# Expert gate and up of a mixture layer: tokens stationary, three passes on halves split on chip, instead of weights stationary in full fp32

## The reference, cut to what matters

```python
def grouped_moe(h, w_router, b_router, w1, w3, w2):      # h: 512 x 1024
    probs = softmax(ht @ w_router)                       # 16 experts
    ...                                                  # two experts and two weights a token
    xs = x_pad[slot_tok].reshape(nblk, MOE_BLOCK, D)     # tokens sorted by expert, padded to blocks
    def expert_block(args):
        xb, e = args
        return (jax.nn.silu(xb @ w1[e]) * (xb @ w3[e])) @ w2[e]
    ys = lax.map(expert_block, (xs, blk_expert)).reshape(P, D) * slot_w[:, None]
    ...                                                  # the two results of a token added
```

## Time and profile before

| | us |
|---|---|
| median of three runs | 3443.12 |
| the profiled execution, its own time | 3443.09 |
| its span from first to last instruction | 3441.1 |
| TensorE busy in the span | 3124.4 (91%) |
| VectorE, ScalarE, GpSimd busy | 1458.3, 1072.6, 1095.8 |
| first product of the expert stage starts, last one ends | 2854.86, 3374.17 |

### The profile page before, as it was taken

How to read it: one execution, slowest core, us unless ns; L and a number is a source line. 1 busy time by engine, 2 the same in 40 slices (tenths; PEclk the granted TensorE clock), 3 DMA queues, 4 the chain that set the end, 5 groups by cost and what they waited for, 6 DMA issues and landing times.

```text
span 3441.1 us, 39144 instructions
## 1 busy us (share of the span) xinstructions
PE 3124.4 (91%) x15510; PEld 2408.1 (70%) x15510; DVE 1458.3 (42%) x2548; ACT 1072.6 (31%) x1673; POOL 1095.8 (32%) x538
## 2 busy tenths in 40 slices
PE   4987999999889789899997999989999968999995
PEld 2664777887666567688775777867777737888883
DVE  6677663212156757332203456647673251000003
ACT  3454324223245432422314442223442230000002
POOL 1331343444323224344443553434543401000001
PEclk8998999999999889999998999999999988999997
DMA  5210553433321036374232226343332308888883
GB/s 210 61 50 25 184 191 104 137 127 94 99 86 51 30 125 206 110 293 135 92 105 79 83 66 243 121 115 110 110 105 86 110 0 319 334 331 335 337 320 110
DMA packets 186037, 501.21 MB, mean 146 GB/s; under 512 B 19408, under 2 KB 101456, under 8 KB 175648
## 3 DMA queue, kind: packets, MB, share of 16 engines
q1 hardware_dynamic: 162192, 415.14, 36.0%
q0 software_dynamic: 13200, 49.32, 3.6%
q10 hardware_dynamic: 10496, 34.71, 2.9%
HBM read 463.83 MB, written 35.29 MB: 145 GB/s over the span
## 4 chain that ended last, share of the span: by engine, by line
PE 76%; DVE 12%; ACT 4%; DMA 3%; issue 2%; POOL 1%; ACTq 1%; DVEq 0%; POOLq 0%; SPq 0%
PE banks L664 18%; PE banks L666 18%; PE banks L665 18%; PE banks L1241 9%; PE banks L1263 5%; PE banks L721 2%; PE banks L756 1%; PE banks L746 1%; DVE arena L2110 1%; DVE arena L2109 1%; PE banks L767 1%; DVE abuf L1961 1%; DMA abuf<-in_pos 1%; PE banks L727 1%; DVE abuf L2052 1%
## 5 line engine op out<-in xcount | busy, mean ns | idle before, releaser
L2632 POOL TENSOR_TENSOR w_lo<-ring,w_hi 128x1024 fp32r<-128x1024 f32 (+1 forms) x379 | 918.4, 2426 | 1499.1 <-ACT w_hi L1357 1499.0
L665 PE MATMUL banks<-h_lo,w_hi 128*128 128x512 f32 x2104 | 835.1, 397 | 0.0
L664 PE MATMUL banks<-hx_hi,w_hi 128*128 128x512 f32 (+2 forms) x1400 | 584.0, 417 | 54.2 <-DVE h_lo L1913 31.8
L1357 ACT ACTIVATE w_hi<-ring 128x1024 fp32r<-128x1024 f32 (+1 forms) x379 | 393.4, 1040 | 603.9 <-DMA ring<-in_w_all 515.4
L666 PE MATMUL banks<-hx_hi,w_lo 128*128 128x512 f32 (+2 forms) x1400 | 555.3, 397 | 0.0
L665 PEld LDWEIGHTS banks<-h_lo,w_hi 128*128 128x128 f32 x2104 | 401.7, 191 | 94.0 <-issue 8.2
L664 PEld LDWEIGHTS banks<-hx_hi,w_hi 128*128 128x128 f32 (+2 forms) x1400 | 268.8, 192 | 153.6 <-issue 79.6
L1241 PE MATMUL banks<-abuf,ring 128*128 128x128 f32 x2944 | 335.3, 276 | 1.8 <-DVE abuf L2583 1.8
L1241 PEld LDWEIGHTS banks<-abuf,ring 128*128 128x128 f32 x2944 | 333.1, 193 | 2.3 <-ACT abuf L1820 1.2
L666 PEld LDWEIGHTS banks<-hx_hi,w_lo 128*128 128x128 f32 (+2 forms) x1400 | 267.5, 191 | 60.4 <-issue 0.3
L664 PE MATMUL banks<-hf_hi,w_hi 128*128 128x512 f32 x704 | 278.3, 395 | 14.3 <-DVE h_lo L1913 14.3
(11 more groups left out here) (384 smaller groups left out, 4549.0 us busy)
## 6 DMA issues: line engine op xcount, KB each, us to landing
ring<-in_w_all SPq DMA_DIRECT2D x356, 512.0 KB, 3.9
ring<-in_w_all SPq DMA_DIRECT2D x46, 2048.0 KB, 8.4
arena<-in_w_all SPq DMA_DIRECT2D x26, 2048.0 KB, 8.4
arena<-in_w_all SPq DMA_DIRECT2D x80, 512.0 KB, 5.3
abuf<-in_w_all SPq DMA_DIRECT2D x48, 512.0 KB, 4.9
routed<-abuf POOLq DMA_DIRECT2D x1, 12288.0 KB, 50.6
abuf<-routed POOLq DMA_DIRECT2D x23, 512.0 KB, 8.5
made<-abuf POOLq DMA_DIRECT2D x23, 512.0 KB, 7.9
```

The lines of the kernel that those rows point to most:

```text
L664: pe.matmul(bank[0:m, :], upper, hi, start=first, stop=False)
L665: pe.matmul(bank[0:m, :], upper, lo, start=False, stop=False)
L1357: act.activation(w_hi[s][:, 0:n], raw_w[s][:, 0:n], ACT.Copy).then_inc(w_upper, 1)
L2632: pool.tensor_tensor(w_lo[s][:, 0:n], raw_w[s][:, 0:n], w_hi[s][:, 0:n], ALU.subtract)\
```

## The change

Gate and up get the tokens as the stationary operand and the weights as the moving one. Both are split on chip into a high and a low fp32r half, and each of the eight chunks of the width is three products with 512 moving columns (`gate_or_up`). Results are now token by feature, so the product of silu(gate) and up (`hid_tok`) is turned by four transposes of TensorE (`turn_hidden`) and copied to `hidb` by VectorE before the down product. A matrix of gate or up arrives as two loads of 1 MB, each into a slot of its own (four slots; two of them where `moe` and `h` lie). ScalarE writes the high half of a slot in two instructions of 128 x 1024, VectorE the low half over the raw weights in two more. A slot is loaded again when TensorE has used it (`unit_used`). Down weights have two buffers. TensorE's order becomes gate, up, rows_in(b + 1), down(b - 1), turn_hidden(b). The turned rows, too, are split (two ScalarE copies, two VectorE subtractions) and have one buffer pair instead of two. GpSimd's code is unchanged.

```diff
+            def gate_and_up(b, first=False):
+                e = expert(b)
+                for u in range(4):
+                    if not first:
+                        sp.wait_ge(sem("unit_used"), 4 * b + (u - 3))
+                    half = u % 2
+                    sp.dma_start(slot_raw[u], part_of(e, u // 2)[:, half * (SLOT // 2):(half + 1) * (SLOT // 2)])\
+                        .then_inc(w_in[u], 16)
...
-            expert_slot(0, 0, ring[0], "wg_in")
-            expert_slot(0, 1, ring[1], "wu_in")
-            with sp.Fori(1, N_BLK) as b:
-                expert_slot(b, 0, ring[0], "wg_in", sem("g_done"), b)
-                expert_slot(b - 1, 2, wdown, "wd_in", sem("d_done"), b)
-                expert_slot(b, 1, ring[1], "wu_in", sem("u_done"), b)
-            expert_slot(N_BLK - 1, 2, wdown, "wd_in", sem("d_done"), N_BLK)
+            sp.wait_ge(sem("htok_done"), 2 * QT)
+            gate_and_up(0, True)
+            down_in(0, 0)
+            gate_and_up(1)
+            gate_and_up(2)
+            down_in(1, 1)
+            with sp.Fori(0, (N_BLK - 3) // 2) as i:
+                for n in range(2):
+                    b = 2 * i + (n + 3)
+                    gate_and_up(b)
+                    down_in(b - 1, n, b - 1)
+            down_in(N_BLK - 1, 0, N_BLK - 1)
...
-            def up_products(w, par, bank, signal):
-                for ct in range(4):
-                    for k in range(KC):
-                        mm = pe.matmul(bank[:, ct * P:(ct + 1) * P],
-                                       w[:, k * E_FF + ct * P:k * E_FF + (ct + 1) * P],
-                                       xT[par][:, k * P:(k + 1) * P], start=(k == 0), stop=(k == KC - 1))
-                mm.then_inc(sem(signal), 1)
...
+            def gate_or_up(b, which):
+                if which == 0:
+                    pe.wait_ge(sem("xTd_done"), 2 * b + 2)
+                for n in range(8):
+                    u, k = 2 * which + n // 4, n % 4
+                    if k % 2 == 0:
+                        pe.wait_ge(w_lower, 8 * b + (STREAM.n_split + 4 * which + n // 2 + 1))
+                    upper, lower = slot_hi[u][:, k * E_FF:(k + 1) * E_FF], slot_lo[u][:, k * E_FF:(k + 1) * E_FF]
+                    rows_hi, rows_lo = xT_hi[:, n * P:(n + 1) * P], xT_lo[:, n * P:(n + 1) * P]
+                    pe.matmul(lin[which], rows_hi, upper, start=(n == 0), stop=False)
+                    pe.matmul(lin[which], rows_hi, lower, start=False, stop=False)
+                    mm = pe.matmul(lin[which], rows_lo, upper, start=False, stop=(n == 7))
+                    if k == 3:
+                        mm.then_inc(sem("unit_used"), 1)
+
+            def turn_hidden(b):
+                pe.wait_ge(sem("hidden"), b + 1)
+                for k in range(4):
+                    mm = pe.transpose(aux[:, k * P:(k + 1) * P], hid_tok[:, k * P:(k + 1) * P], ident)
+                mm.then_inc(sem("hidden_turned"), 1)
...
                 for n in range(2):
-                    b, par = 2 * i + (n + 1), (n + 1) % 2
+                    b = 2 * i + (n + 1)
                     pe.wait_ge(sem("silu_read"), b)
-                    gate_block(b, par)
-                    down_block(b - 1)
+                    gate_or_up(b, 0)
+                    gate_or_up(b, 1)
                     rows_in(b + 1)
-                    up_block(b, par)
-            down_block(N_BLK - 1)
+                    down_block(b - 1, n)
+                    turn_hidden(b)
+            down_block(N_BLK - 1, 0)
...
             def step(b, par, first=False):
                 act.wait_ge(sem("hidden"), b)
                 gate_half(b)
+                upper_weights(b + 1, (0, 1))
+                upper_rows(b + 1)
+                upper_weights(b + 1, (2, 3))
                 made_half(b - 1, 1 - par, first)
-                rows_half(b + 1, 1 - par)
...
+            def lower_weights(b, units):
+                for u in units:
+                    for half in range(2):
+                        cols = slice(half * UNIT, (half + 1) * UNIT)
+                        dve.wait_ge(w_upper, 8 * b + (STREAM.n_split + 2 * u + half + 1))
+                        TT(slot_lo[u][:, cols], slot_raw[u][:, cols], slot_hi[u][:, cols], SUB).then_inc(w_lower, 1)
...
             def block_step(b, par, first=False):
+                lower_weights(b + 1, (0,))
+                gated_block(b)
+                lower_weights(b + 1, (1,))
+                lower_rows(b + 1)
+                lower_weights(b + 1, (2, 3))
                 made_half(b - 1, 1 - par, first)
-                rows_half(b + 1, 1 - par)
-                gated_block(b)
+                hidden_turned(b)
```

More of the change, by code:

```diff
@@ L452, in two_blocks @@
         flat = lambda v: v.rearrange("p a b -> p (a b)")
+        hid_tok = abuf[:, 11, :]
         xr, hidb = flat(abuf[:, 0:2, :]), abuf[:, 6, :]
-        xT = [flat(abuf[:, n:n + 2, :]) for n in (2, 4)]
+        xT_hi, xT_lo = halves("xT_hi", "abuf", 2 * SEQ, D), halves("xT_lo", "abuf", 4 * SEQ, D)
+        down = [wdown, flat(merged2)]
+        SLOT = 4 * UNIT
+        slot_raw = [whole_ring[:, 0:SLOT // 2], whole_ring[:, SLOT:SLOT + SLOT // 2], flat(moe)[:, 0:SLOT // 2],
+                    flat(h)[:, 0:SLOT // 2]]
+        slot_lo, slot_hi = ([halves("slot_%s%d" % (name, n), *at, SLOT // 2) for n, at in enumerate(
+            (("ring", skip), ("ring", SLOT + skip), ("arena", shared_end + skip), ("h", skip)))]
+            for name, skip in (("lo", 0), ("hi", SLOT // 2)))
         yb = [flat(abuf[:, n:n + 2, :]) for n in (7, 9)]
@@ L1263, in down_block @@
                         mm = pe.matmul(sc_b[half], hidb[:, k * P:(k + 1) * P],
-                                       wdown[:, k * D + half * SEQ:k * D + (half + 1) * SEQ],
+                                       down[par][:, k * D + half * SEQ:k * D + (half + 1) * SEQ],
                                        start=(k == 0), stop=(k == 3))
@@ L1815, in _, with upper_rows, upper_weights @@
                         .then_inc(sem("htok_done"), 1)
-            def rows_half(b, par):
+            def upper_rows(b):
                 act.wait_ge(sem("rows_turned"), b + 1)
-                act.activation(xT[par][:, 0:SEQ], pt_b[0], ACT.Copy).then_inc(sem("xTa_done"), 1)
+                for half in range(2):
+                    act.activation(xT_hi[:, half * SEQ:(half + 1) * SEQ], pt_b[half], ACT.Copy).then_inc(sem("xTa_done"), 1)
+            def upper_weights(b, units):
+                for u in units:
+                    act.wait_ge(w_in[u], 16 * b + (STREAM.landed[u] + 16))
+                    for half in range(2):
+                        cols = slice(half * UNIT, (half + 1) * UNIT)
+                        act.activation(slot_hi[u][:, cols], slot_raw[u][:, cols], ACT.Copy).then_inc(w_upper, 1)
             def gate_half(b):
-                act.wait_ge(sem("g_done"), b + 1)
+                act.wait_ge(sem("unit_used"), 4 * b + 2)
                 act.activation(sg[0][:, :], lin[0], ACT.Silu).then_inc(sem("silu_read"), 1)
@@ L1830, in made_half @@
                 act.activation(yb[par][:, 0:SEQ], sc_b[0], ACT.Copy).then_inc(sem("ya_done"), 1)
-            rows_half(0, 0)
+            upper_rows(0)
+            upper_weights(0, range(4))
             gate_half(0)
-            rows_half(1, 1)
+            upper_rows(1)
+            upper_weights(1, range(4))
             def step(b, par, first=False):
@@ L2578, in _, with lower_rows, hidden_turned @@
             mine.restart()
-            def rows_half(b, par):
-                dve.wait_ge(sem("rows_turned"), b + 1)
-                dve.tensor_copy(xT[par][:, SEQ:], pt_b[1]).then_inc(sem("xTd_done"), 1)
+            def lower_rows(b):
+                for half in range(2):
+                    cols = slice(half * SEQ, (half + 1) * SEQ)
+                    dve.wait_ge(sem("xTa_done"), 2 * b + (half + 1))
+                    TT(xT_lo[:, cols], pt_b[half], xT_hi[:, cols], SUB).then_inc(sem("xTd_done"), 1)
+            def lower_weights(b, units):
+                for u in units:
+                    for half in range(2):
+                        cols = slice(half * UNIT, (half + 1) * UNIT)
+                        dve.wait_ge(w_upper, 8 * b + (STREAM.n_split + 2 * u + half + 1))
+                        TT(slot_lo[u][:, cols], slot_raw[u][:, cols], slot_hi[u][:, cols], SUB).then_inc(w_lower, 1)
             def gated_block(b):
                 dve.wait_ge(sem("silu_read"), b + 1)
-                dve.wait_ge(sem("u_done"), b + 1)
-                TT(hidb, sg[0][:, :], lin[1], MUL).then_inc(sem("hidden"), 1)
+                dve.wait_ge(sem("unit_used"), 4 * b + 4)
+                TT(hid_tok, sg[0][:, :], lin[1], MUL).then_inc(sem("hidden"), 1)
+            def hidden_turned(b):
+                dve.wait_ge(sem("hidden_turned"), b + 1)
+                dve.tensor_copy(hidb, aux).then_inc(sem("hidden_in"), 1)
             def made_half(b, par, first=False):
@@ L2594, in made_half @@
```

(21 more changed lines are left out.)

43 lines of the change are left out of this document (22 added, 21 removed).

## The result

The changed kernel takes 3423.55 us (median of 12 runs, 3416.35 to 3434.6) against 3443.47 (12 runs) for the kernel before: ratio 0.9942, 95% interval 0.9933 to 0.9951. That is 20 us or 0.58% faster, where 3427 in a range of 3401 to 3466 had been forecast. The profiled execution's span went from 3441.1 to 3421.8 us, 19.3 us less.

What follows compares the result with a forecast made beforehand. TensorE bounds the changed stage, transfers 11% behind; after the change a chain through the row load would. 21 x (21.1 - 22.04) = -19.7, start +3, end +0.5: -16.2 us against 3443.09, forecast 3427, range 3401 to 3466.

Steps and rivals of the forecast that it cites:

- TensorE's own block: TensorE's work per block in the expert stage: gate and up, rows, down and transposes, 19.3 us, 2.7 less than before.
- The chain: Expert stage, gate(b) to gate(b + 2) through subtractions, down-result copy, store and row load: 42.15 us, 21.1 a block; chance 0.60.
- The 7.3: The chain's term for landing of weight unit 1 after its issue: 7.3 us, between ends of 5.4 and 8.4.
- The clock leaves 1.00 in the stage: Listed sign that the prediction is wrong: TensorE's granted clock falls below full speed in the expert stage.
- The start: Before the stage's 21 counted blocks: later rows, splitting and a falling clock add 3 us, from 0 to 7.
- The end: Before the last down product: turning and copying lie bare where 0.90 us of waiting stood, +0.5 us.
- the border of 17: Whole kernel: a difference up to 0.5%, 17 us, counts as "same"; the forecast stood just inside.
- TensorE stays the bound: Rival: TensorE's 19.3 us decides each block of the expert stage, giving 3389 us; chance 0.12.
- The transfers set the pace as they flow now: Rival: expert-stage transfers stay at 333 GB/s, a block stays at 22.04 us, giving 3447; chance 0.10.
- The 3415: Estimate for the sum if transfers at about 358 GB/s, a core's share, made a block 20.5 us.
- The row load is starved: Rival: the row load beside units 0 and 1 takes 13.8 us, a block 23.7, giving 3481; chance 0.13.
- a border of 11.6: Row load time in us from which the starved row load decides; a block of 22.7 us gives +17.

Runs made afterwards that it cites:

- rows_first: The changed kernel with GpSimd loading the rows of block b + 2 before it stores the results of block b - 1; 3390.97 us, ratio 0.9843.
- swap_only: The changed kernel without the splitting: gate and up are single fp32 products of 512 columns on raw weights, tokens stationary; 3445.51 us, ratio 1.0006.
- made_early: The changed kernel with VectorE's copy of the down result moved ahead of the last two weight subtractions; 3390.27 us, ratio 0.9843.
- one_down: The changed kernel with one buffer of down weights, loaded when the down product before has ended; 3508.91 us, ratio 1.0181.
- rows_first_two: rows_first without the pass on the tokens' low half in gate and up, so the product is incomplete; 3345.63 us, ratio 0.9711.

## Why the prediction was right

**TensorE's own block.** Forecast 19.3 us, measured 19.37 in rows_first. The passes follow at 0.233 us (forecast 0.228), and swap_only confirms from the other side that the gain is in the passes and not in the orientation.

**VectorE and ScalarE.** A subtraction of 1024 columns takes 1.22 us (forecast 1.23), a rounding 1.06 (1.06).

```profile
L2645 DVE TENSOR_TENSOR slot_lo<-ring,slot_hi x92: 1217/1220/1227, 2853.0 to 3319.9; 128x1024 fp32r<-128x1024 f32 x92
```

Beside GpSimd's issues no subtraction of the changed kernel is slower than 1.23 us. The same holds in rows_first, where the row load is issued in their midst. The Trainium skill (SBUF — State Buffer, "SBUF: two separate sides") infers that descriptor making does not contend with a two-input operation; the subtractions' side of that is now seen here.

**The chain.** On the two blocks shown, from the start of a gate at 3054.35: the copy of the down result begins at S + 21.6 and ends at S + 22.3, where the prediction had 24.0; unit 1 had landed 5.9 us after its issue instead of 7.3 (in the block after it took 8.1, and the copy ended at S + 23.9). The 7.3 itself was added up 0.2 us too high: S + 2, 8.0 and 2.6 us are S + 12.6. The issue follows in 1.43 us (1.44). From its issue to TensorE's start on the rows it is 9.57 us (8.5). The 8.2 us of rows, down and turning are as forecast. The sum is 41.5 us against 42.15: two terms off by 1.8 and 1.1 us in opposite directions. Over the stage a block is 21.04 us against 21.1. made_early, rows_first and one_down, which each change one link of the chain, all moved the way that the chain says; one_down moved twice as far as expected, because there the chain closes in one block instead of two.

**What was off.** "The clock leaves 1.00 in the stage" was on my list of what would prove me wrong, and it did, in four blocks, for about 1.7 us each, 0.3 us a block. TensorE's waits were 25.1 us in 21 blocks, 1.2 a block instead of 1.8. 19.37 + 1.2 + 0.3 is 20.9 of the 21.04. The rest is what a stop costs beside its wait: a block with a wait and no fall of the clock is some 0.2 us longer than 19.4 plus its wait (21.41 with one of 1.81, 20.81 with one of 1.21), and thirteen of the 21 blocks have one, 0.13 us a block. The right total for a block is thus partly luck: the waits were smaller, and the clock's fall took up half of the difference. The start cost 4.6 us where I had taken 3 in a span of 0 to 7. The end cost 0.2 instead of 0.5.

**Sign and size.** The stage gained the 16.2 us that the sum gave. That the figures agree to the tenth is luck too: the blocks gained 1.3 us more than forecast, and start and end together cost 1.3 more. The median moved by 20 us, past the border of 17 (the interval is 17 to 23 us), so "faster" came true, at a chance of 0.40 against 0.42 for "same". The forecast lay at the border, and the chances said so. By the profiles the stage alone would have stayed just short of it; the 3.1 us ahead of it made the difference.

**The rivals.** "TensorE stays the bound" was wrong for the change but became true with one swap of two lines: made_early and rows_first land at 3390 and 3391, where that rival had 3389. "The transfers set the pace as they flow now" is refuted by the change itself, at 347 GB/s, and more so by rows_first_two: 423 GB/s over 300 us. The Trainium skill (HBM Reference, "Specifications"), whose core's share of about 358 GB/s I weighed, also says that a core streaming alone measures about 425; this case agrees with the latter. (The 3415 that I put beside that share would have needed a shorter chain as well, since the chain's 21.1 us are over the 20.5 of such transfers.) "The row load is starved" did not come with the change (9.0 us against a border of 11.6), but one_down shows that it exists: with 12.5 us the kernel is slower than before.

## What to carry to other kernels

When an engine gets new work in its program, look at what stands behind that work in its list and who outside waits for it: here a copy behind the splitting held a store, the store held a load on GpSimd's queue, and the load held TensorE. A prefetch should be issued from the event that frees its buffer and never from behind a store that has nothing to do with it. An average of 57% for an engine says nothing about such a chain; adding it up from one event to its return two blocks later does.

## What the runs showed of the hardware

- How long a load takes from issue to landing goes with what was issued just before it, and not with how full the engines are on average: the same 512 KB took 7.6 us (made_early, DMA share 0.94), 9.0 (the change, 0.88), 10.4 (rows_first, 0.97, issued at most 0.3 us behind 2 MB) and 12.5 (one_down, 0.74, issued some 2 us behind 2 MB and right behind the store) in the median. Within the changed kernel a lag of 0.35 us or more behind a load of 1 MB went with 8.4 to 9.8 us instead of 6.8 to 7.4. The longest but one of these medians cost nothing, as that load was asked for early.
- Of TensorE's waits in the stage, those of up to 2.15 us were followed by no fall of the granted clock. Of the five of 2.34 to 2.47 us four were, and the next 16 instructions took 8.6 to 8.7 us instead of 7.03; the fifth, of 2.43 us, was not. In one_down every wait was 3.0 us or more, and the clock was lower behind each. I had counted only the waits.
- 300 us of loads of 1 and 2 MB, row loads and stores together ran at 423 GB/s with the DMA share at 1.01. So loads of 1 MB, with 8 KB a partition, do not keep the engines from that rate; no run has the same bytes in loads of 2 MB beside it.
